# Two mixer stacks on one core: a folded spectral transform, two weight slabs whose low parts are made by adding transfers, and a new order of work around the convolution

## What is computed

```
def fnet_heads(a, fnet_map):
    a4 = a.reshape(bsz, seq, A_HEADS, A_HEAD_DIM).astype(jnp.float32)
    f = jnp.fft.fft2(a4, axes=(1, 3), norm="ortho").real.astype(a.dtype)
    y = jnp.einsum("bshd,hde->bshe", f, fnet_map)

def conformer_conv_heads(v, gate, conv_w, conv_b, ln_g, ln_b):
    u = v * jax.nn.sigmoid(gate)
    u = depthwise convolution of 31 taps along seq (u, conv_w) + conv_b
    u = layernorm(u per head of 128, ln_g, ln_b)
    return jax.nn.silu(u)

p = h @ w_in_ab            # 512 spectral, 512 values, 512 gates
y = concatenate([fnet_heads(p[..., :512], fnet_map), conformer_conv_heads(...)]) @ w_out_ab
```

## Time and profile before

| | us |
|---|---|
| median of 3 runs | 729.29 (729.09 to 730.04) |
| the profiled execution | 732.02 |
| its span from first to last instruction | 730.2 |
| PE busy | 714.9 (98%) |
| DVE busy | 502.5 (69%) |
| ACT busy | 394.4 (54%) |
| 16 DMA engines, hardware queue | 54.6% of their span |
| mean granted TensorE clock | 0.995 |

### The profile page before, as it was taken

The page is one execution under the profiler, slowest core; times in us unless marked ns, Lnnn a source line. Parts: engine busy times, 40 slices in busy tenths (PEclk is TensorE's granted clock), DMA queues, the critical chain, the costliest instruction groups (busy, mean ns, idle before and its releaser), DMA issues.

```text
span 730.2 us, 9502 instructions
## 1 busy us (share of the span) xinstructions
PE 714.9 (98%) x3804; PEld 620.6 (85%) x3804; DVE 502.5 (69%) x801; ACT 394.4 (54%) x610; POOL 2.4 (0%) x8
## 2 busy tenths in 40 slices
PE   7999999999999999999999999999999999999996
PEld 5878889889999999888888888888888888888885
DVE  5689996998977889987744545455686445555544
ACT  3156635964886776768644344443666443344423
POOL 0000000000000000000000000000000000000000
PEclk9999999999999999999999999999999999999998
DMA  8999994799836342433755545554326455455201
GB/s 335 415 423 373 423 401 166 260 376 347 355 117 230 118 173 91 176 139 115 289 183 207 187 173 189 206 180 173 116 116 230 179 201 197 174 182 206 74 1 57
DMA packets 23084, 156.11 MB, mean 214 GB/s; under 512 B 2560, under 2 KB 2816, under 8 KB 5120
## 3 DMA queue, kind: packets, MB, share of 16 engines
q1 hardware_dynamic: 22464, 152.88, 54.6%
q0 software_dynamic: 576, 2.62, 0.9%
HBM read 154.44 MB, written 1.05 MB: 213 GB/s over the span
## 4 chain that ended last, share of the span: by engine, by line
PE 91%; DMA 4%; ACT 2%; DVE 1%; SPq 0%; issue 0%; ACTq 0%
PE pb L1602 24%; PE pb L1604 23%; PE pb L1603 23%; PE pb L1671 10%; DMA raw<-w_dram 4%; PE pb L1913 2%; PE pb L2019 1%; PE pb L2087 1%; PE pb L1941 1%; DVE raw L1033 1%; ACT t L751 1%; ACT w L635 0%; ACT r L748 0%; PE pb L1830 0%; PE pb L1811 0%; PE pb L1891 0%
## 5 line engine op out<-in xcount | busy, mean ns | idle before, releaser
L1030 DVE TENSOR_TENSOR w<-raw,w 128x2048 fp32r<-128x2048 f32 x97 | 221.2, 2289 | 140.7 <-ACT w L635 140.7
L635 ACT ACTIVATE w<-raw 128x2048 fp32r<-128x2048 f32 x97 | 184.8, 1914 | 143.2 <-PE pb L1604 114.7
L1602 PE MATMUL pb<-w,r 128*128 128x512 f32 (+1 forms) x608 | 239.1, 393 | 1.9 <-ACT f L759 1.7
L1604 PE MATMUL pb<-w,r 128*128 128x512 f32 (+1 forms) x608 | 235.5, 387 | 0.0
L1603 PE MATMUL pb<-w,r 128*128 128x512 f32 (+1 forms) x608 | 235.1, 387 | 0.0
L1602 PEld LDWEIGHTS pb<-w,r 128*128 128x128 f32 x608 | 114.2, 188 | 24.8 <-issue 2.1
L1604 PEld LDWEIGHTS pb<-w,r 128*128 128x128 f32 x608 | 114.2, 188 | 23.8
L1603 PEld LDWEIGHTS pb<-w,r 128*128 128x128 f32 x608 | 114.3, 188 | 22.3
L1602 PE MATMUL pb<-r,w 128*128 128x256 f32 x288 | 82.4, 286 | 0.0
L1604 PE MATMUL pb<-r,w 128*128 128x256 f32 x288 | 81.5, 283 | 0.0
L1603 PE MATMUL pb<-r,w 128*128 128x256 f32 x288 | 81.5, 283 | 0.0
(11 more groups left out here) (208 smaller groups left out, 663.3 us busy)
## 6 DMA issues: line engine op xcount, KB each, us to landing
raw<-w_dram SPq DMA_DIRECT2D x129, 1024.0 KB, 4.9
ow<-w_dram SPq DMA_DIRECT2D x8, 1024.0 KB, 15.2
ow<-w_dram SPq DMA_DIRECT2D x8, 512.0 KB, 17.1
oh<-w_dram SPq DMA_DIRECT2D x2, 1024.0 KB, 23.6
x<-x_dram SPq DMA_DIRECT2D x2, 512.0 KB, 5.8
f<-rc_dram POOLq DMA_DIRECT2D x1, 1024.0 KB, 5.0
acc<-row_dram POOLq DMA_DIRECT2D x2, 512.0 KB, 6.1
out_dram<-f SPq DMA_DIRECT2D x4, 256.0 KB, 2.3
```

The costliest lines, as they stand in the source:

```text
L635: return e.activation(out, in_, ACT.Copy, **kw)
L1030: return e.tensor_tensor(out, a, b, op)
L1602: e.matmul(out, a_hi, b_hi, start=start, stop=False)
L1604: return e.matmul(out, a_lo, b_hi, start=False, stop=stop)
```

## The change

**Fold.** The transform over 128 of a real signal is symmetric: only 64 + 1 cosines and 63 sines differ. The constant `cdsd` becomes 128 wide, with the cosines in columns 64 to 127 and 0 and the sines in columns 1 to 63 (column 0 is frequency 64, column 64 is frequency 0). The first transform is then one 128-column matmul for each head and half, two heads sharing a bank; the second multiplies each block by the sequence cosines and by the sequence sines, for 130 of the 256 sequence positions, into two places of one bank; ACT puts the rows together with three copies; the map takes positions 0 to 129 with maps whose rows are summed with a mirrored map, and positions 130 to 255 with the sums under a sign (`sqt`) and the stored positions read backwards. POOL makes these two sets of maps from `fmap`, a mirrored map loaded behind `dft` and a sign column.

**Adding transfers.** For slabs 26 and 27 DVE makes no low part. ACT writes the rounded slab a second time, negated, into the low half, and POOL issues a transfer of the slab from DRAM that adds to it. PE waits for that transfer. The raw buffer is free after ACT's second copy.

**Orders.** ACT streams slabs 26 and 27 one by one around the copies of a0 to a3, 28 after the diagonals, 29 after the root of tile 3. DVE takes the taps of all tiles to their end before the inverse of tile 3, and slab 28's and 29's low parts after it. PE takes the means of tiles 0 and 1 ahead of `both(2)`.

**Banks.** `o.n += 4` goes, and the first transform uses four banks where it used eight, so the values and what follows up to the first transform move by four banks.

```diff
@@ outputs()
-    o.n += 4
@@
-    for h in range(4):
-        o.out(("ac", h, 0), ("ac", h, 1))
+    for g in range(2):
+        o.out(("ac", g, 0), ("ac", g, 1))
+BY_DMA = [26, 27]
@@ SP: what a raw buffer waits for
-                    emptied.append((s_lo, n_mat))
+                    k = n_mat - 1
+                    emptied.append((s_minus, BY_DMA.index(k) + 1) if k in BY_DMA else (s_lo, LOW_AT[k]))
@@ POOL
             e.wait_ge(s_mv, 12)
-            e.dma_start(acc[0][:, :], dft_d).then_inc(s_dft, 16)
+            e.dma_start(acc[0][:, :], dft_d[:, 0:4 * T]).then_inc(s_dft, 16)
+            e.wait_ge(s_na, 7)
+            for i in range(2):
+                e.dma_start(sqt[i][:, :], dft_d[:, 4 * T + i * T:5 * T + i * T]).then_inc(s_mir, 16)
+            e.wait_ge(s_mir, 32)
+            for i in range(2):
+                e.tensor_scalar(sqt[i][:, :], sqt[i][:, :], sgn, None, MUL).then_inc(s_fold, 1)
+            for i in range(2):
+                part = C("fmap", i * T, T)
+                e.tensor_tensor(part, part, sqt[i][:, :], ADD).then_inc(s_fold, 1)
+            for i in range(2):
+                e.tensor_scalar(sqt[i][:, :], C("fmap", i * T, T), sgn, None, MUL).then_inc(s_fold, 1)
+            def low_sum(k):
+                e.wait_ge(s_minus, BY_DMA.index(k) + 1)
+                e.dma_start(W[(k + 2) % NSPL][:, 1, :], w_d[MATS[k]], accum_op=ADD).then_inc(s_sum[k], 16)
+            low_sum(26)
+            low_sum(27)
             e.wait_ge(s_flo, 4)
@@ ACT
+                    if k in BY_DMA:
+                        copy(W[(k + 2) % NSPL][:, 1, 0:n], raw_of(i)[:, 0:n], scale=-1.0).then_inc(s_minus, 1)
@@
-            for c in range(2):
-                fill(24 + c)
-                for d in (2 * c, 2 * c + 1):
+            def spectral(*ds):
+                for d in ds:
                     p.wait_ge(*ended("a", d))
                     copy(F2[:, d, :], out_of("a", d)).then_inc(s_a, 1)
+            stream(MATS[26])
+            spectral(0, 1)
+            stream(MATS[27])
+            diagonals(0, 1, 2)
+            spectral(2, 3)
@@
-                copy(F2[:, 4 + h, :], out_of("f", h)).then_inc(s_f, 1)
-                if h < 3:
-                    diagonals(2 * h, 2 * h + 1)
+                cosines, sines = [bank_of("f", h)[:, o_:o_ + NS] for o_ in (0, T)]
+                copy(F2[0:64, 4 + h, 0:NS], sines[0:64, :]).then_inc(s_sin, 1)
+                copy(F2[64:128, 4 + h, 0:NS], cosines[64:128, :])
+                p.wait_ge(s_sin, h + 1)
+                copy(F2[0:1, 4 + h, 0:NS], cosines[0:1, :]).then_inc(s_f, 1)
@@
-            diagonals(*range(6, 16))
-            fill(25)
-            diagonals(*range(16, 31))
+            diagonals(*range(3, 31))
+            stream(MATS[28])
@@
             ln_root(3)
-            fill(26)
+            stream(MATS[29])
             ln_high(3)
@@ DVE
-            pump(36)
-            fill(24)
-            pump(20)
+            pump(46)
@@
-            fill(25)
@@
-            pump(3)
+            pump(78 - tap_n["n"])
             ln_centre(3)
-            pump(9)
+            pump(len(taps) - tap_n["n"])
             ln_inverse(3)
-            pump(85 - tap_n["n"])
+            ln_centre(0)
+            ln_centre(1)
             ln_scale(3)
-            pump(4)
+            stream(MATS[28])
             ln_low(3)
-            pump(4)
-            for d in range(3):
-                ln_centre(d)
-            fill(26)
+            ln_centre(2)
+            stream(MATS[29])
@@ PE
+                if k in BY_DMA:
+                    p.wait_ge(s_sum[k], 16)
@@
-                    e.matmul(out_of("ac", h, a), F2[:, h, a * P:(a + 1) * P], C("cdsd"), start=True,
-                             stop=True).then_inc(s_ps, 1)
+                    for b in range(2):
+                        h = 2 * g + b
+                        p.wait_ge(s_a, h + 1)
+                        done = e.matmul(out_of("ac", g, a)[:, b * P:b * P + P], F2[:, h, a * P:(a + 1) * P], C("cdsd"),
+                                        start=True, stop=True)
+                    done.then_inc(s_ps, 1)
@@
-                    e.matmul(out, AC[:, h, a, 0:P], acc[0][:, a * T:a * T + T], start=a == 0, stop=False)
-                    done = e.matmul(out, AC[:, h, a, P:256], acc[0][:, (2 + a) * T:(3 + a) * T], start=False,
-                                    stop=a == 1)
+                    e.matmul(bank_of("f", h)[:, 0:NS], col, acc[0][:, a * T:a * T + NS], start=a == 0, stop=False)
+                    done = e.matmul(bank_of("f", h)[:, T:T + NS], col, acc[0][:, (2 + a) * T:(2 + a) * T + NS],
+                                    start=False, stop=a == 1)
@@
-                e.matmul(out_of("fm", h), C("fmap", h * P, P), F2[:, 4 + h, :], start=True,
+                e.matmul(out_of("fm", h)[:, 0:NS], C("fmap", h * P, P), F2[:, 4 + h, 0:NS], start=True, stop=False)
+                e.matmul(out_of("fm", h)[:, NS:T], sqt[h // 2][:, h % 2 * P:h % 2 * P + P], F2[:, 4 + h, T - NS:0:-1], start=False,
                          stop=True).then_inc(s_ps, 1)
@@
             ln_row(3)
-            both(2)
             ln_mean(0, (s_tap, tap_at[0, 30]))
             ln_mean(1, (s_tap, tap_at[1, 30]))
+            both(2)
```

## The result

| | before | after |
|---|---|---|
| median, us | 729.45 (6 runs) | 727.04 (6 runs, 726.74 to 727.91) |
| ratio, 95% interval | | 0.9965 [0.9955, 0.9976] |
| the profiled execution, us | 732.02 | 727.91 |
| its span | 730.2 | 726.1 |
| predicted | | 725.3 (723.8 to 728.0) |

What follows compares the result with a forecast made beforehand. PE was taken to bound the kernel, with DVE nearly as full around the edit. 5.13 us saved on PE less 1.15 waiting for DVE's taps gave 3.96 off the median of 729.29: 725.3 us, range 723.8 to 728.0.

Steps and rivals of the forecast that it cites:

- the forecast's own 724.3 to 726.5: Whole kernel: the main case around 725.3 us, given a chance of 0.62.
- PE, removed work: Both transforms on PE: shorter matmuls save 1.73 us in the first and 3.40 in the second, 5.13 in all.
- The reversed operand: PE's map matmuls reading positions backwards: taken as 0 us, at most +0.9.
- ACT: Second transform: three copies a head take 0.85 us, at most 1.25, just keeping pace with PE's 0.88.
- The wait the change makes: PE at the row of tile 3: waits 1.15 us for DVE's inverse behind the taps, capping the gain.
- 15 taps, 5.94: End of DVE's tap list, before tile 3's inverse: 15 taps at 0.396 us each, ending at 311.1.
- After the taps: PE from the row of tile 3 to k-tile 4: 12.26 us as before, k-tile 4 starting 3.96 us earlier.
- The adding transfers: Low parts of slabs 26 and 27: priced near 5.0 us, costing nothing; up to 15.4 each would fit.
- The banks: Values and first transform: moving the ring by four banks costs 0, since PE shows no gap there.
- Late transfers: Rival at the first k-tiles: PE waits from 15.4 us each; chance 0.10 of over 0.2% slower, 0.05 within.
- POOL and DVE met: Rival in the attention: POOL's six operations hold up DVE, 2.0 us; with other small losses 726.5 to 727.8, chance 0.15.
- The rival in which DVE does not hold PE: Row of tile 3: taps end before PE arrives, all 5.13 us are kept, 723.8 us; chance 0.08.

Runs made afterwards that it cites:

- the taps in turn: The changed kernel with the taps of the three tiles taken in turn from the first on; 726.53 us, ratio 0.9948.
- the best order: The changed kernel with taps taken in turn, tile 3's inverse six taps before their end, means between k-tile 2's halves; 725.31 us, ratio 0.9938.
- the fold alone: The changed kernel without adding transfers, with DVE's list and the means' place of before; fold, banks and ACT's order stay; 729.38 us, ratio 0.9994.
- the transfers alone: The kernel before plus only the two adding transfers and ACT's negated copies, all orders and the full transform as before; 729.67 us, ratio 0.9995.
- the low parts on DVE: The changed kernel without adding transfers, DVE making the low parts of slabs 26 and 27 after the first 33 taps; 731.59 us, ratio 1.0024.

## Why the prediction was right, and where it was off

The sign, the mechanism and the range came as written. The size did not: 727.04 lies outside the forecast's own 724.3 to 726.5, in the band that was kept for a smaller gain from other causes.

- **PE, removed work.** 4.94 us to the row of tile 3 (33.61 before, 28.67 after without the wait; the kernels without it have 28.68), 5.13 forecast. Matmuls of 128 and 130 columns run at 0.222 to 0.225 us each. The reversed operand costs nothing: the 126 columns read backwards and the 130 forwards both start 0.22 us apart.
- **ACT.** Three copies a head took 3.53 us for four heads, 0.88 a head, where 0.85 was taken; PE did not wait, and the convolution followed the map at once. The row is of ACT's timeline of the kernel after:

```profile
283.48 3.53 ACT L665 ACTIVATE f<-pb 64x130 f32<-64x130 f32 x12 [0.42 <-PE pb L1942]
```

- **The wait the change makes** was named with its place and its releaser. Its size was the step that failed. DVE's list was right up to the centring of tile 3: 303.75, where 304.8 was forecast, in an execution that reached the first transform 1.08 us sooner. Then came "15 taps, 5.94", with a tap priced at 0.396 ("Taps have one price all over the trace"). A tap that needs the tap just before it costs 0.52, and the last eight are all of tile 2. The kernel before showed it too, four such taps in 2.04 us, twice, in the rows below, (2.04 - 0.48)/3 = 0.52 each; the prediction read only the 33 in 13.14. The term was 6.94, and 1.0 us of the gain went with it; the taps in turn gave it back. With the taps at their forecast price the wait would have been 1.96 - 1.0 = 0.96, and the sum 4.94 - 0.96 = 3.98.

```profile
316.11 2.04 DVE L1033 SCALAR_TENSOR_TENSOR f<-f,vec 128x256 f32<-128x256 f32 x4
...
318.40 2.04 DVE L1033 SCALAR_TENSOR_TENSOR f<-f,vec 128x256 f32<-128x256 f32 x4
```

- **After the taps.** 323.44 - 311.23 = 12.21 us, 12.26 forecast.
- **The adding transfers.** Taken at 5.0 us or a little more, they cost 14.0 and 15.0, nearer the far end of 17.8 and just under the 15.4 each from which the sum would have suffered one after the other. They ran beside each other, so 9 us of slack were left. The slack carried the step, not the price; that part was luck. The Trainium skill (Collectives: The Full Stack, the section on the bandwidth ceiling) states its rule of two source reads for the add of a ReduceScatter; the estimate of 10 us taken from it was nearer than the row, and still short by 2.5 us for a transfer alone.
- **The banks.** Right in the sum and wrong in the reason. "PE shows no gap there" was false: PE waited 1.72 us for ACT ahead of the values. The move took that wait away, and 1.0 us of it came back as a wait for DVE at the queries and 0.7 between the scores and the first transform.
- **The whole.** 3.03 us in the section, less 0.3 in K (166.2 for 165.9), is 2.7; timed, 2.4, with an interval of 1.8 to 3.3. What is left between 2.7 and 2.4 is below what these runs can tell.
- **The rivals.** Late transfers did not come. POOL and DVE met, as that rival had it, but the price fell on POOL and 0.16 us on DVE, not six times 0.42. The smaller gain that it forecast, 726.5 to 727.8, came all the same, by another cause: the last eight taps. The rival in which DVE does not hold PE is what the best order makes true: M falls by 5.0 us (45.87 to 40.84), and the ratio is 0.9938, some 4.5 us.

## What to carry to other kernels

When two engines are both full in a stretch, work taken from one is worth only what is taken from the other as well: here the fold alone and the transfers alone gave nothing, and together, in a new order, they gave 2.4 us. Price repeated instructions by the pace of those that follow their own result and of those that don't, and let chains take turns. When a wait is made, look whether its producer must stand at the end of its engine's list: with one reciprocal six taps further forward, and the scaling behind it ahead of two centrings, the last 0.8 us of PE's wait went.

## What was not expected of the hardware

- A DVE multiply-add of 128 x 256 lasts 0.48 us; the next one starts after 0.396 if it waits for one further back, and after 0.52 if it waits for this one. Two chains taken in turn are enough: the first taps alternate between two tiles and keep 0.396. The Trainium skill (VectorE: DVE Perf Modes, The DRAIN you can't avoid) has the next operation start only when the pipe is empty, and finds no cost of a semaphore behind each operation, though it adds that an operation that is not held starts earlier. Here such neighbours overlap by 0.08 us, the wait for the neighbour costs 0.12, and the measurement decides.
- An adding transfer of 1 MB took 12.5 us alone and 14.0 and 15.0 as a pair, a plain one of the same size on the same queue 5.1. The pair slowed others: the slab loads issued between 272 and 300 us landed in 11.5 us (median of three), where they take 4.9 in the kernel before and with a single adding transfer. No later work was near enough to feel it.
- An operation of POOL that met a DVE operation with two inputs in SBUF took 2.53 us instead of 0.73; the DVE operation kept its 2.28.
- PE's wait of 3.08 us was followed by the lower clock level, with slow products until about 319 us, and one of 1.80 us, in the kernel after, was not (granted clock 1.00 throughout). A wait of PE on DVE can so cost about twice its length. With the low parts on DVE a wait of 2.86 us did the same (granted clock 0.50 from 310 to 315 us), and there the slow products ran in time in which PE would have waited anyway. Four waits of up to 1.10 us, in the fold alone, left the clock at 1.00.
